# A two-block transformer and state-space kernel on one core: first modulation computed in pairs of inner tiles, local state-space outputs ahead of the carried ones, skip product on ScalarE

## The reference

```
# first block, each layer
mod = silu(c) @ ada_w + ada_b             # 6 x 1024 values, for tokens and for context
u   = rms_norm(h, g_mix) * (1 + sc1) + sh1
q, k, v = split(u @ w);  q, k = rms_norm per head;  attention;  h += ga1 * (y @ wo)
h  += ga2 * squared_relu_mlp(rms_norm(h, g_mlp) * (1 + sc2) + sh2)

# second block, first layer: the state-space layer
u = rms_norm(h, a_norm) @ w_in
s[t] = a_bar * s[t-1] + b_bar @ u[t]      # 64 groups of 16 features, 64 complex states each
y = real(c @ s) + d_skip * u
g = gelu(y);  h += val * sigmoid(gate), where val, gate = split(g @ w_glu)
# then a gated convolutional FFN, stick-breaking attention, and an FFN again
```

## Time and profile before

| | us |
|---|---|
| median of three runs | 1752.43 |
| lowest, highest | 1748.91, 1753.97 |
| the profiled execution | 1750.73 |
| its span, first to last instruction | 1748.9 |
| TensorE busy | 1627.1 |
| VectorE busy | 1312.5 |
| ScalarE busy | 870.6 |
| GpSimd busy | 96.5 |

### The profile page before, as it was taken

The page is one execution under the profiler, slowest core; times in us unless marked ns, Lnnn a source line. Parts: engine busy times, 40 slices in busy tenths (PEclk is TensorE's granted clock), DMA queues, the critical chain, the costliest instruction groups (busy, mean ns, idle before and its releaser), DMA issues.

```text
span 1748.9 us, 32745 instructions
## 1 busy us (share of the span) xinstructions
PE 1627.1 (93%) x11892; PEld 1435.7 (82%) x11892; DVE 1312.5 (75%) x2239; ACT 870.6 (50%) x1497; POOL 96.5 (6%) x152
## 2 busy tenths in 40 slices
PE   5899999899999999698989999689999989799999
PEld 3677866688888888584789999689999988599999
DVE  4899797788767877678677786777887666468874
ACT  4555387343213433556555555155555576455552
POOL 0001030000000023100001212100000000000000
PEclk9899999999999999898999999799999999899999
DMA  9236651435657855320256768525555544045554
GB/s 359 87 108 228 217 140 43 145 119 187 200 192 239 264 177 167 106 94 13 66 183 203 220 200 304 234 97 174 186 180 192 183 143 145 1 156 180 182 192 142
DMA packets 79626, 290.74 MB, mean 166 GB/s; under 512 B 10000, under 2 KB 11792, under 8 KB 77600
## 3 DMA queue, kind: packets, MB, share of 16 engines
q1 hardware_dynamic: 69120, 249.03, 43.0%
q0 software_dynamic: 10400, 40.30, 7.0%
HBM read 270.61 MB, written 18.68 MB: 165 GB/s over the span
## 4 chain that ended last, share of the span: by engine, by line
PE 75%; DVE 14%; ACT 6%; issue 4%; DMA 2%; ACTq 0%; DVEq 0%; SPq 0%; POOLq 0%
PE bank L699 21%; PE bank L701 21%; PE bank L700 21%; DVE stat L2069 2%; PE bank L764 1%; PE bank L766 1%; PE bank L765 1%; ACT w_hi L1127 1%; DVE w_lo L1554 1%; DVE prob L2088 1%; DMA raw<-weights 1%; PE bank L909 1%; PE bank L920 1%; PE bank L777 1%; PE bank L933 1%
## 5 line engine op out<-in xcount | busy, mean ns | idle before, releaser
L699 PE MATMUL bank<-u_hi,w_hi 128*128 128x256 f32 (+1 forms) x1936 | 616.5, 318 | 36.3 <-DVE u_lo L1887 25.6
L700 PE MATMUL bank<-u_lo,w_hi 128*128 128x256 f32 (+1 forms) x1936 | 604.6, 312 | 0.0
L701 PE MATMUL bank<-u_hi,w_lo 128*128 128x256 f32 (+1 forms) x1936 | 604.3, 312 | 0.0
L1554 DVE TENSOR_TENSOR w_lo<-raw,w_hi 128x1024 fp32r<-128x1024 f32 x372 | 452.2, 1222 | 175.8 <-ACT w_hi L1127 163.3
L1127 ACT ACTIVATE w_hi<-raw 128x1024 fp32r<-128x1024 f32 x360 | 375.9, 1050 | 173.7 <-PE bank L701 144.6
L699 PEld LDWEIGHTS bank<-u_hi,w_hi 128*128 128x128 f32 x1936 | 376.6, 195 | 63.1 <-issue 39.2
L700 PEld LDWEIGHTS bank<-u_lo,w_hi 128*128 128x128 f32 x1936 | 376.6, 195 | 22.0 <-issue 3.0
L701 PEld LDWEIGHTS bank<-u_hi,w_lo 128*128 128x128 f32 x1936 | 376.1, 194 | 19.0
L699 PE MATMUL bank<-hid_hi,w_hi 128*128 128x512 f32 (+1 forms) x512 | 174.0, 340 | 0.0
L701 PE MATMUL bank<-hid_hi,w_lo 128*128 128x512 f32 (+1 forms) x512 | 172.1, 336 | 0.0
L700 PE MATMUL bank<-hid_lo,w_hi 128*128 128x512 f32 (+1 forms) x512 | 172.1, 336 | 0.0
(11 more groups left out here) (319 smaller groups left out, 2278.0 us busy)
## 6 DMA issues: line engine op xcount, KB each, us to landing
raw<-weights SPq DMA_DIRECT2D x372, 512.0 KB, 3.4
ada_raw<-ada_w SPq DMA_DIRECT2D x80, 512.0 KB, 4.2
ada_first<-ada_w SPq DMA_DIRECT2D x16, 512.0 KB, 15.5
bias_sb<-bias_na POOLq DMA_DIRECT2D x16, 256.0 KB, 3.3
toep_dram<-zeros POOLq DMA_DIRECT2D x8, 512.0 KB, 8.9
bat_dram<-bat POOLq DMA_DIRECT2D x16, 256.0 KB, 4.1
ca_dram<-ca POOLq DMA_DIRECT2D x16, 256.0 KB, 3.7
s_bat<-bat_dram POOLq DMA_DIRECT2D x4, 1024.0 KB, 7.5
```

The lines of the kernel that those rows point to most:

```text
L699: pe.matmul(dst, wh, hi[:, kt, xs], start=first, stop=False)
L700: pe.matmul(dst, wh, lo[:, kt, xs], start=False, stop=False)
L701: return pe.matmul(dst, wl, hi[:, kt, xs], start=False, stop=final)
L1554: TT(w_lo[:, slot, :], raw[:, slot, :], w_hi[:, slot, :].bitcast(F32), ALU.subtract).then_inc(S["lo"], 1)
```

## The change

- The first modulation is computed in four parts of four columns: shift and scale of inner tiles 2n and 2n+1. The DMAs of `x` (in four pieces), of the first part's matrices and of the first three weight units come first, then the other three parts; the fourth part takes the first one's buffer and waits for its body.
- TensorE does all eight row sums, then the first body and total, then both silu rows. The other three bodies and totals stand in `first_tiles` of qk0, ahead of inner tiles 1, 3 and 5. ScalarE copies them in its norm loop ahead of inner tiles 2, 4 and 6; VectorE adds bias and forms the gain at the same places (`first_mod`). All bodies use one bank.
- On ScalarE the 18 power copies come ahead of the root, the first total's copy and the first silu row behind it, then the first three weight splits. On VectorE 14 small table operations move from ahead of the root to behind the norm.
- In win VectorE evicts a tile ahead of the next `w_lo` instead of behind it, with the late norm ahead of both at the first tile.
- The state update on VectorE works on the real and imaginary part in one instruction where it can.
- The local output products are issued ahead of the wait for the states, and those of the second half ahead of the turning of the first. The skip product moves from POOL (two instructions of 1024 columns) to ScalarE (eight of 256).

```diff
             sp.dma_start(vec[:, :], vecs).then_inc(vec_in, 16)
-            sp.dma_start(h[:, :, :], x_t).then_inc(x_in, 16)
             sp.dma_start(con[:, 0:N_EARLY], cons[:, 0:N_EARLY]).then_inc(early_in, 16)
-            for n in range(16):
-                sp.dma_start(ada_first[n // 8][:, n % 8, :], ada_w[n]).then_inc(ada_first_in[n // 4], 16)
+            for n in range(4):
+                sp.dma_start(h[:, 2 * n:2 * n + 2, :], x_t[:, 2 * n:2 * n + 2, :]).then_inc(x_in[n], 16)
...
+            def load_first_ada(n):
+                if n == 3:
+                    sp.wait_ge(ada_first_done, 1)
+                for c, m in enumerate((2 * n, 2 * n + 1, 8 + 2 * n, 9 + 2 * n)):
+                    sp.dma_start(ada_first[n][c][:, :], ada_w[m]).then_inc(ada_first_in[n], 16)
+            load_first_ada(0)
+            for g in range(3):
+                sp.dma_start(raw[:, g, :], weights[g]).then_inc(raw_in[g], 16)
+            for n in range(1, 4):
+                load_first_ada(n)
...
                 for kt in range(KT):
+                    if s.name == "qk0":
+                        if kt in (1, 3, 5):
+                            first_ada(1 + kt // 2)
+                            first_total(1 + kt // 2)
...
                 pe.wait_ge(ada_first_in[n], 64)
-                ada_body([ada_first[n // 2][:, n % 2 * 4 + c, :] for c in range(4)], TILE[n])
+                ada_body([ada_first[n][c][:, :] for c in range(4)], TILE[3])
...
                 if n:
-                    pe.wait_ge(ada_first_sum, n)
+                    pe.wait_ge(S["mod"], CREDIT + n)
...
             pe.wait_ge(early_in, 16)
-            first_rows(range(0, 3))
+            first_rows(range(KT))
...
             first_ada(0)
-            first_rows(range(3, 6))
-            first_ada(1)
-            silu_rows(0)
-            first_rows(range(6, KT))
-            first_ada(2)
-            for n in range(3):
-                first_total(n)
-            first_ada(3)
-            silu_rows(1)
-            first_total(3)
+            first_total(0)
+            for c in range(2):
+                silu_rows(c)
...
-            def ssm_outputs(k):
+            def ssm_sites(k, a):
+                for k4 in range(4):
+                    for hf in range(2):
+                        gl = 2 * a + hf
+                        yield (2 * k + k4 // 2, k4, k4 % 2 * 8 + gl, hf * 64,
+                               psum[4 + 2 * k + hf][k4 * NCH:(k4 + 1) * NCH, a * P:(a + 1) * P])
+            def ssm_local(k):
...
                     pe.wait_ge(tab_in[q], 32)
+                for a in range(4):
+                    for q, k4, g, hb, dst in ssm_sites(k, a):
+                        pe.matmul(dst, u_g[:, k, g % 8, k4, :], TOEP_TAB[q][:, g, :], start=(a == 0), stop=False,
+                                  skip_group_check=True)
+            def ssm_carried(k):
+                for q in (2 * k, 2 * k + 1):
...
                 for a in range(4):
-                    for part in range(3):
-                        for k4 in range(4):
...
-                                if part == 0:
-                                    mm = pe.matmul(dst, u_g[:, k, gl, k4, :], TOEP_TAB[q][:, g, :], start=True, stop=False,
-                                                   skip_group_check=True)
-                                else:
-                                    mm = pe.matmul(dst, H_ST[q][hb:hb + 64, part - 1, jj, :],
-                                                   CA_TAB[q][hb:hb + 64, jj, part - 1, :], start=False, stop=(part == 2),
-                                                   skip_group_check=True)
+                    for ri in range(2):
+                        for q, k4, g, hb, dst in ssm_sites(k, a):
+                            mm = pe.matmul(dst, H_ST[q][hb:hb + 64, ri, g // 2, :], CA_TAB[q][hb:hb + 64, g // 2, ri, :],
+                                           start=False, stop=(ri == 1), skip_group_check=True)
...
                 ssm_states(q)
-            for k in range(2):
-                ssm_outputs(k)
-                ssm_turn_y(k)
+            ssm_local(0)
+            ssm_carried(0)
+            ssm_local(1)
+            ssm_turn_y(0)
+            ssm_carried(1)
+            ssm_turn_y(1)
...
                     act.wait_ge(ada_first_sum, n)
-                A(ada_sb[:, :], TILE[n][:, 0:P], ACT.Copy).then_inc(ada_first_copied, 1)
+                A(ada_sb[:, :], TILE[3][:, 0:P], ACT.Copy).then_inc(ada_first_copied, 1)
...
                 A(sq[:, kt % 2, :], h[:, kt, :], ACT.Square).then_inc(ss0, 1)
-            for n in range(3):
-                first_copy(n)
-            act.wait_ge(n_v, 1)
-            root(rsn[:, :], ssum[:, :]).then_inc(n_rs, 1)
-            silu_row_copy(0)
...
             last.then_inc(pre_e, 1)
-            first_copy(3)
+            act.wait_ge(n_v, 1)
+            root(rsn[:, :], ssum[:, :]).then_inc(n_rs, 1)
+            first_copy(0)
+            silu_row_copy(0)
...
                 for kt in range(KT):
+                    if k == 0 and kt in (2, 4, 6):
+                        first_copy(kt // 2)
...
+            act.wait_ge(ssm_tu, 4)
+            for k in range(2):
+                for t in range(4):
+                    last = A(u_sc[:, k, :, t, :], u_sc[:, k, :, t, :], ACT.Copy, scale=VC("a_d", 4 * k + t))
+                last.then_inc(ssm_skip, 1)
...
                     for jj in range(body):
+                        if s.kind == "IN":
+                            if i * body + jj == 0:
+                                late_norm(LATE[s.name])
+                            tile(s, i, jj, body, first)
+                            lower(s.unit0 + jj + 3, i, per)
+                            continue
...
+            def first_mod(n):
+                dve.wait_ge(ada_first_sum, n + 1)
+                part = [t[:, 0, 0:16, :].rearrange("p (a k) c -> p a k c", a=2)[:, :, 2 * n:2 * n + 2, :] for t in (mod, adab)]
+                TT(part[0], ADA_BANK[:, 8 * n:8 * n + 8].rearrange("p (a k c) -> p a k c", a=2, k=2), part[1],
+                   ALU.add).then_inc(S["mod"], 1)
+                dve.wait_ge(S["mod"], CREDIT + n + 1)
+                a = VEC["g_mix"][0] + 4 * n
+                STT(gain[:, 0, 0, 2 * n:2 * n + 2, :], mod[:, 0, 8 + 2 * n:10 + 2 * n, :], 1.0,
+                    vec[:, a:a + 4].rearrange("p (k c) -> p k c", c=2), ALU.add, ALU.mult).then_inc(gain_done, 1)
+                dve.wait_ge(gain_done, n + 1)
...
                     if kt < KT:
+                        if k == 0 and kt % 2 == 0:
+                            first_mod(kt // 2)
...
-            link(TS(v(14), pr_[:, 1, :], -1.0, None, ALU.add))
...
-            link(TT(v(16), v(18), v(15), ALU.mult))
...
             dve.wait_ge(adab_in, 16)
-            dve.wait_ge(ada_first_sum, 4)
-            TT(mod[:, 0, 0:16, :], ADA_BANK[:, 0:32].rearrange("p (m c) -> p m c", c=2), adab[:, 0, 0:16, :],
-               ALU.add).then_inc(S["mod"], 4)
...
             norm(0, "mix0")
+            link(TS(v(14), pr_[:, 1, :], -1.0, None, ALU.add))
...
+            link(TT(v(16), v(18), v(15), ALU.mult))
...
                 js = slice(q * QJ, (q + 1) * QJ)
-                vr, vi, rr = (rot[:, k, js, :] for k in range(3))
+                rr = rot[:, 2, js, :]
+                vr, vi = (rot[:, k, js, :].unsqueeze(1).to_broadcast([P, 2, QJ, NCH]) for k in range(2))
                 xs = psum[q][:, :].rearrange("p (j r c) -> p r j c", j=QJ, r=2)
-                xr, xi = x_mod[:, 0], x_mod[:, 1]
-                gr, gi = g_st[:, 0], g_st[:, 1]
-                hr, hi = H_ST[q][:, 0, :, to], H_ST[q][:, 1, :, to]
...
                 dve.memset(H_ST[q][:, :, :, 0:1].rearrange("p a j c -> p (a j) c"), 0.0)
-                TT(xr, xs[:, 0], vr, ALU.mult)
-                m1 = mark(TT(x_tmp[:, 0], xs[:, 1], vi, ALU.mult))
-                TT(xi, xs[:, 1], vr, ALU.mult)
-                m2 = mark(TT(x_tmp[:, 1], xs[:, 0], vi, ALU.mult))
+                TT(x_mod[:, :], xs, vr, ALU.mult)
+                link(TT(x_tmp[:, :], xs, vi, ALU.mult))
+                m1 = mark(TT(x_mod[:, 0], x_mod[:, 0], x_tmp[:, 1], ALU.add))
+                m2 = mark(TT(x_mod[:, 1], x_mod[:, 1], x_tmp[:, 0], ALU.subtract))
                 until(m1)
-                m1 = mark(TT(xr, xr, x_tmp[:, 0], ALU.add))
+                dve.tensor_tensor_scan(flat(g_st[:, 0]), flat(rr), flat(x_mod[:, 0]), 0.0, ALU.mult, ALU.add)
                 until(m2)
-                m2 = mark(TT(xi, xi, x_tmp[:, 1], ALU.subtract))
-                until(m1)
-                m1 = mark(dve.tensor_tensor_scan(flat(gr), flat(rr), flat(xr), 0.0, ALU.mult, ALU.add))
+                link(dve.tensor_tensor_scan(flat(g_st[:, 1]), flat(rr), flat(x_mod[:, 1]), 0.0, ALU.mult, ALU.add))
+                m1 = mark(TT(g_tmp[:, :, :, fr], g_st[:, :, :, fr], vi[:, :, :, fr], ALU.mult))
+                m2 = mark(TT(H_ST[q][:, :, :, to], g_st[:, :, :, fr], vr[:, :, :, fr], ALU.mult))
```

(53 more changed lines are left out.)

5 lines of the change are left out of this document (removed).

## The result

| | before | after |
|---|---|---|
| median (lowest to highest), 20 runs each | 1750.71 us (1748.26 to 1753.97) | 1754.63 us (1752.86 to 1760.14) |
| profiled execution, its span | 1750.73, 1748.9 | 1755.86, 1754.1 |

Ratio 1.0025, interval 1.0018 to 1.0032: about 4.4 us slower, which is a difference, but less than the 0.3% that was set as the bound of "same". The forecast was 1758.9 in a range of 1749 to 1766, that is +6.5 us for the change itself.

The account below looks back on a forecast made before the run. TensorE was taken as the bound, busy 1627 of 1748.9 us, except in the front and state-space stretches. Front +13.5 and state space -7.0 give +6.5, on a median of 1752.43: 1758.9 us, range 1749 to 1766.

Parts of the forecast that it names:

- same: Outcome for the whole kernel's time: within about 0.3% (5.3 us), between 1747.2 and 1757.7 us; chance 0.36.
- small operations, w_lo ahead of the copy: Front, VectorE: 14 small operations now behind the norm, 3.3 us, of which 2.2 is covered by the wait for tile 0.
- Part 1: Front: rearranged row sums, copies and silu rows bring the first product from 44.02 to 36.7, -7.3 us; bounds -6 to -8.5.
- Part 2: First tiles: three bodies between products cost +6.0 us, three TensorE waits for VectorE's u_lo, 3.3 each, +9.9.
- Part 3: First tiles: gaps on TensorE lower its granted clock, +4.6 us, of which 0.7 only uses up cover; bounds 0 to +6.
- Part 4: Win: evicting a tile ahead of the next w_lo lets the turns start earlier, -1.9 us; bounds -1.2 to -3.
- Part 5: State space: skip product off POOL removes VectorE's 4.60 us add, -4.3 us; bounds -4.3 to 0.
- Part 6: State space, VectorE: merged state operations leave a quarter at 5.1 us, gain 0; bounds +-0.3 per quarter.
- Part 7: State space: local products ahead of the states shorten the second half until VectorE's gelu chain bounds, -0.8 us; bounds 0 to -1.6.
- State space in all: Win and state space together: -1.9-4.3-0.8 = -7.0 us; bounds -2 to -10.
- The rival of a late DMA in front: Front: bodies still hold the first tile because DMA is late; no size given, no chance of its own (the rest: 0.05).
- The rival 1744.1 (hidden hand-over): First tiles: TensorE finds u_lo ready when a body ends, so only bodies cost; -8.3 us in all; chance 0.13.

Follow-up runs that it names:

- e5: Changed kernel with eight extra 512-column products into an unused bank behind each of the three totals in the first tiles; 1751.55 us, ratio 1.0001 to the kernel before.
- e8: Changed kernel with x loaded again as one 2 MB DMA ahead of the constants; 1758.14 us, ratio 1.0039 to the kernel before.
- e2: Kernel before with only the front's edits (inner-tile pairs, order of row sums, DMAs and small operations); 1762.07 us, ratio 1.0060.
- e4: Changed kernel with VectorE's u_lo of inner tiles 1, 3, 5 ahead of the next pair's modulation; 1749.58 us, ratio 0.9987 to the kernel before.
- e3: Changed kernel with the skip product back on POOL as two multiplications; 1759.55 us, ratio 1.0047 to the kernel before.
- e1: Kernel before with only the edits of win and the state-space layer; 1745.20 us, ratio 0.9966.
- e6: Changed kernel with e4's order, second and third bodies ahead of the first product, fourth ahead of inner tile 1; 1737.59 us, ratio 0.9920 to the kernel before.
- e7: e6 with VectorE's state update in its old twelve operations per quarter; 1735.86 us, ratio 0.9909 to the kernel before.

## Why the prediction was right, step by step

The time was 1754.63 against a forecast of 1758.9, which is 4.3 us too high and inside the range. The hand-overs, the clock and the skip product acted as named. The number is helped by luck: errors of up to 2.2 us cancel, as the sum below shows. By the forecast's own bound of 0.3% (1757.7) the time is "same", which had 0.36, and not "slower", which had 0.52. In front:

| term | forecast | measured | how read |
|---|---|---|---|
| earlier first product | -7.3 | -9.47 | 34.55 against 44.02 |
| three bodies | +6.0 | +5.9 | 3 x 1.96, apart from the clock |
| three hand-overs | +9.9 | +8.8 | 3 x 2.95, e.g. 56.29-51.39-1.96 |
| small operations, w_lo ahead of the copy | +1.1 | +1.7 | product stretches of e5 (4.10+4.31+4.30+7.14) against 18.18 |
| clock | +3.9 | +5.4 | +0.7 for the first body (2.63 for 1.96), 4.8 in products against e5 |
| copy of tile 0 | +13.5 | +12.4 | 74.56 against 62.20; the forecast has another -0.1, for products that leave the slow start |

- Part 1: the rearranged row sums, copies and silu rows did what was worked out. What was missed is the 2.16 us of x's load. With it put back (e8) the first product is 7.61 earlier than before, against the 7.3 forecast.
- Part 2: the mechanism was right, and every hand-over was ended by u_lo as named. The size was 0.35 too high each: from ScalarE's copy to VectorE's add it is 0.76 (41.36 to 42.12) and not 0.9, and the product starts 0.04 behind the end of u_lo (44.20) and not 0.2.
- Part 3: the low clock was real and cost somewhat more than forecast. The +4.6 was a choice between 0 and the 5.9 of three times 1.97, not a sum. Behind the first hand-over the 18 products took 7.15 us up to the next body, 14 of them wholly or partly at half clock, against 4.31 in e5; the next 18 took 5.93 against 4.30. The 0.7 of the first body was in no term of the forecast; it belongs to the long wait ahead of the first product and not to the hand-overs, and `e2` and `e4` do not have it.
- Part 4, win: mis-sized. Forecast -1.9, measured -0.75 at the turns. The last tile did go ahead of the last w_lo. But it stands behind the w_lo of 1114.19, which is 13.21 later than the one of 1100.98 before, where the delay had been 12.06: 1.15 of the 1.9 is lost here. This w_lo waited 1.75 for w_hi, and this (1113.10) 2.46 for the DMA of its weight. SP issues that DMA when an earlier w_lo is done, the one of 1098.81, and this one is 13.33 later than the 1085.48 before, because it now stands behind a tile's eviction. The forecast had put the price of later w_lo at nothing up to 0.5, looking only at TensorE; what it missed is that a later w_lo also asks for a weight later. In the other seven kernels with this order the turns gain 0.5 to 1.3. In `e2`, with the old order, they lose 1.5, so this stretch varies too. Another 1.1 between the turns and the first x_mod is luck of the clock, as said above.
- Part 5, skip: -4.3 forecast, from an add that ends 0.3 and not 0.2 after POOL's pair; the long add fell from 4.60 to 0.42, and e3 loses 3.9 again by the times. The cover on ScalarE was there: its eight products end at 1124.6, long before 1144.37.
- Part 6, merged states: forecast 0 per quarter; a quarter takes 5.25 from start to start (1123.35, 1128.63, 1133.88, 1139.14) against 5.13: some +0.5 over the four, inside the bounds.
- Part 7, local first: forecast -0.8, measured -0.69, read from the first gelu input (6.46) to the last u_lo (5.77). It fits the reason given: VectorE's copy at 1148.82 now waits only 0.38 in place of 1.11. No run has this part alone.
- State space in all: -7.0 forecast, -6.3 by the trace, -6.0 by e1's time. Without the 1.1 of the clock the trace gives -5.2.

The errors of front and state space (-2.2 for x's load, -1.1 for the hand-overs, +1.5 for the clock, +0.6 for the small operations, +0.7 for the state space) nearly cancel, and 0.3 more is gone between the copy of tile 0 and the state space: the delay behind the state space is +5.8 where +6.5 was forecast. At the end it is +5.2; on the way it had been 7.1, by steps of the kind described above, so this last 0.6 is not the prediction's merit or fault. For the profiled execution 1757.2 was forecast and 1755.86 measured. The other 3 us of the 4.3 are the step from there to a median: the old kernel's, taken from 3 runs as 1752.43, is 1750.71 over 20, and the new one's is 1.2 below its profiled execution.

The rival of a late DMA in front did not happen: none of the four bodies waits for its matrices in the changed kernel. The rival 1744.1 (hidden hand-over) did not happen either, but e6 and e7 show its point: with the hand-over really hidden the kernel takes 1737.59 and 1735.86, less than the rival's figure.

## What to carry to other kernels

- Where work is cut into pieces so that the consumer can start earlier, look at what the producer's engine does in order: three pieces here cost 8.8 us of waiting and 5.4 of clock, for a start 9.5 earlier. Swapping two steps of VectorE made the loss of 4.4 us a gain of 2.3 against the old kernel, and putting the pieces where TensorE had waited anyway made the gain 16 (each with the state space's 6 in it).
- When a step that frees a buffer is put behind another one, follow the buffer to its next load: here a w_lo 1.3 us later made a weight land late enough to take 1.15 of a gain of 1.9.
- Price an engine's move off POOL or onto it by the row of the VectorE instruction that overlaps it, not by POOL's time alone; and price each DMA that is split or moved for the small loads on the other queue as well.

## What was not expected of the hardware

- A small load on the software queue landed earlier when 2 MB on the hardware queue behind vec were four DMAs behind con rather than one ahead of it: first use at 6.02 against 8.18 before and 7.73 in e8. Whether the split or the order does it was not taken apart. The first product does not follow every tenth of it: `e2` has sv at 5.49 and its first product at 34.63, the changed kernel 6.02 and 34.55.
- Waits of 2.16 us on TensorE, each behind a short total and a wait of 0.4, were followed by a lower granted clock (0.50 in 44 to 50, 0.84 in 50 to 60), those of 1.04 to 1.07 were not (1.00 in e4), nor those of 0.20 to 0.24 (e5). How long it stayed low differed: the three groups of products behind the waits lost 2.8, 1.6 and, as far as it reached the copy of tile 0, 0.3 us against e5.
- A VectorE add with both inputs in SBUF lasts until POOL's pair has ended although it is recorded 0.5 us ahead of it, in all three kernels that have the pair (1114.52 in the earlier trace rows, 1128.19 in e2, 1124.64 in e3, the last with different code around it). The Trainium skill, "SBUF — State Buffer", section "Who interferes with whom", has the order of issue decide which of the two is blocked. By the recorded starts (0.49, 0.49 and 0.50 us) that did not hold here. What the chip does in that half microsecond, no row shows, nor how exact a start recorded on POOL is.
